# Expert gates of a product-key layer: each token's gates built once for all 128 second keys beside the first product's blocks, instead of twice for 64 keys each

## Chip, cores, metric

One NeuronCore of a Trainium2 chip runs the whole program. The metric is device time in microseconds, the median of three runs; lower is better.

## What is computed

The program is a two-block sequence model on 256 tokens of width 1024, float32. The change touches one part of it, the product-key expert layer ("PEER"), which runs three times: for both token streams in layer 0 and for one in layer 1. For each token and each of 8 heads it finds 16 of 16,384 experts:

```
s = einsum("thpd,hpnd->thpn", q, sub_keys)         # 128 first and 128 second keys
st, it = top_k(s, 16); cand = st[..,0,:,None] + st[..,1,None,:]
best, pos = top_k(cand, 16); e = it0 * 128 + it1 at pos; g = softmax(best)
act = gelu(einsum("thkd,td->thk", u[e], t))
out = einsum("thk,thkd->td", g * act, v[e])
```

## The kernel before

The kernel gathers nothing. It streams all of U and V (128 blocks of 128 experts by 1024 each, 512 KB a block) through a ring of 4 slots, computes the activations of all 16,384 experts for all 256 tokens, multiplies them by gates that are zero except for the chosen experts, and multiplies by V. One run of the layer is one phase of the program, in which each engine has its own instruction list and waits on semaphores:

- **Cells.** `S` holds, per partition (first key), a row per second key `c` and in it 256 tokens. Block `c` of U gives row `c`.
- **Blocks.** ScalarE rounds each block to float32r (`high`, L1870, 3 buffers), another engine subtracts to get the rest (`low`), TensorE multiplies the parts. In U (`up`, L1748 to L1750: 24 matmuls of 256 columns a block) `low` is GpSimd's (L1733); in V (`down`, L1800 to L1804: 12 matmuls of 512 columns) it is VectorE's (L2044), which also splits the cell row (`split`, L2037) after ScalarE rounded it (`weights`, L1925).
- **Gelu.** ScalarE turns the product of each U block into row `c` (`gelu`, L1875), and rounds the next ring block right after it. PSUM banks 4 to 7 take the blocks in turn, so `up` may run at most 4 blocks ahead of it.
- **Top-k.** VectorE finds the 16 experts per head beside the first U blocks. Its scratch lies in the rows 64 to 127 of `S`. TensorE turns the result (first keys, second keys, weights of 128 hits per token) around, `turn_found` at L1776, once after block 39 and once after block 51, and ScalarE copies it to `R` (`keep_found`, L1890).
- **Gates.** A gate matrix of one token is the product of two one-hot matrices over its 128 hits, `hotA` (first keys) and `hotB` (second keys times weight). VectorE makes both (`hot`: L2014 compares second keys, L2017 first keys, L2020 multiplies by the weight), TensorE multiplies (`build`, L1786), VectorE multiplies the cells by the result in PSUM (`gate`, L2030). A group is 8 tokens by 64 second keys, one PSUM bank. The 32 groups of second keys 0 to 63 are built beside U blocks 64 to 127, one before every two blocks. The 32 groups of keys 64 to 127 are built beside V blocks 0 to 63 in the same way, with the same `hotA` made again, because those cells are only ready when U is done.
- **Order.** It is written out by hand: TensorE's list decides which build stands before which block, and each engine's list is in program order. A list that stops at a wait holds everything behind it.

## Time and profile before

| | |
|---|---|
| median of 3 runs | 4347.95 us (4345.4 to 4363.05) |
| the profiled execution | 4347.48 us, its span 4345.6 us |
| TensorE busy | 4012.2 us, 92% |
| VectorE busy | 2377.6 us, 55% |
| ScalarE busy | 1645.8 us, 38% |
| GpSimd busy | 1399.2 us, 32% |
| mean granted TensorE clock | 0.955 of full |

The three runs of the layer take the stretches from about 1335 to 2213 us, 2238 to 3115 us and 3445 to 4323 us of the span. A profile row gives the start and the length of an instruction, the engine, the line of the kernel, the tiles, and in brackets how long the engine sat idle before it and what released it. PE is TensorE's matmul, PEld its weight load, DVE is VectorE, ACT is ScalarE, POOL is GpSimd. A float32 matmul appears as two instructions, and their ends are modelled, so the pace is read from one start to the next. A row of stretches gives the stretch, its length, the busy time (and instructions) of PE, PEld, DVE, ACT and POOL, the granted clock, the DMA share and GB/s.

### The profile page before, as it was taken

Reading aid. Unit: us, or ns where it says so; the run is one execution under the profiler, and the core shown is the slowest. Engines: PE = TensorE matmul, PEld = TensorE weight load, DVE = VectorE, ACT = ScalarE, POOL = GpSimd, SP = SyncE. Lnnn points to the kernel's source line nnn. Section 1 sums busy time; section 2 is a strip of 40 time slices with the busy share of each in tenths; the row PEclk is TensorE's granted clock in tenths of the full one; section 3 lists DMA queues with packets and bytes.
Section 4 is the critical chain, followed back from the end, with each engine's and each line's share of the span. In section 5 each row is a group of like instructions: output and inputs, shape, how many; then the busy total and the mean of one; then the engine's idle time right before and its main releaser. Section 6 shows DMA issues by size and latency. Waiting matters only on the chain. (4 is left out here: it accounts for less than half of the span.)

```text
span 4345.6 us, 71586 instructions
## 1 busy us (share of the span) xinstructions
PE 4012.2 (92%) x25466; PEld 3534.9 (81%) x25466; DVE 2377.6 (55%) x4173; ACT 1645.8 (38%) x2573; POOL 1399.2 (32%) x555
## 2 busy tenths in 40 slices
PE   7997798978988999999989999999788799999998
PEld 7973388967657999988879999888676799998887
DVE  4012413145535766687549466885555295667855
ACT  3532203232324443334544433334433344333344
POOL 5840006400005976300038865000000288660000
PEclk9998899989889999999999999999888899999999
DMA  5565544522004554444645544446421255444454
GB/s 188 179 214 194 193 136 150 167 87 73 24 25 131 165 156 140 136 145 155 193 141 169 161 140 134 144 144 192 140 89 39 88 162 166 141 136 141 145 183 150
DMA packets 168400, 614.28 MB, mean 141 GB/s; under 512 B 18593, under 2 KB 20001, under 8 KB 167969
## 3 DMA queue, kind: packets, MB, share of 16 engines
q1 hardware_dynamic: 168224, 611.88, 45.1%
q8 instruction: 117, 1.92, 0.2%
q14 instruction: 59, 0.48, 0.0%
HBM read 610.76 MB, written 1.05 MB: 141 GB/s over the span
## 5 line engine op out<-in xcount | busy, mean ns | idle before, releaser
L1733 POOL TENSOR_TENSOR ring_r<-ring,ring_hi 128x1024 fp32r<-128x1024 f32 x408 | 1073.2, 2638 | 1435.5 <-ACT ring_hi L1870 1434.8
L1870 ACT ACTIVATE ring_hi<-ring 128x1024 fp32r<-128x1024 f32 x792 | 837.8, 1059 | 822.8 <-DMA ring<-in_peer_v 485.9
L1748 PE MATMUL bank<-H_r,ring_hi 128*128 128x256 f32 x3264 | 938.2, 287 | 65.3 <-POOL ring_r L1733 63.1
L1749 PE MATMUL bank<-H_r,ring_hi 128*128 128x256 f32 x3264 | 925.5, 284 | 0.0
L1750 PE MATMUL bank<-H_r,ring_r 128*128 128x256 f32 x3264 | 925.0, 283 | 0.0
L1748 PEld LDWEIGHTS bank<-H_r,ring_hi 128*128 128x128 f32 x3264 | 627.8, 192 | 73.6 <-POOL ring_r L1733 45.6
L1749 PEld LDWEIGHTS bank<-H_r,ring_hi 128*128 128x128 f32 x3264 | 628.2, 192 | 0.0
L1750 PEld LDWEIGHTS bank<-H_r,ring_r 128*128 128x128 f32 x3264 | 627.8, 192 | 0.0
L1800 PE MATMUL bank<-ring_hi,H_r 128*128 128x512 f32 x1536 | 484.6, 397 | 4.7 <-DVE ring_r L2044 4.6
L280 POOL TENSOR_TENSOR ring_r<-ring,ring_hi 128x1024 fp32r<-128x1024 f32 x133 | 319.2, 2402 | 495.3 <-ACT ring_hi L274 494.8
L1802 PE MATMUL bank<-ring_r,H_r 128*128 128x512 f32 x1536 | 475.6, 391 | 0.0
L1804 PE MATMUL bank<-ring_hi,H_r 128*128 128x512 f32 x1536 | 475.1, 391 | 0.0
L2044 DVE TENSOR_TENSOR ring_r<-ring,ring_hi 128x1024 fp32r<-128x1024 f32 x384 | 467.9, 1219 | 0.0
L290 PE MATMUL bank<-H_r,ring_hi 128*128 128x256 f32 (+1 forms) x1464 | 455.3, 311 | 0.0
L1875 ACT ACTIVATE arena<-bank 128x256 f32 (+1 forms) x384 | 147.6, 384 | 638.3 <-PE bank L1750 637.9
L1786 PEld LDWEIGHTS bank<-arena 128*128 128x128 f32 x3072 | 365.5, 192 | 9.1 <-ACT arena L1875 2.0
L1786 PE MATMUL bank<-arena 128*128 128x64 f32 x3072 | 363.6, 271 | 1.4 <-ACT arena L1875 1.4
L2030 DVE TENSOR_TENSOR arena<-arena,bank 128x512 f32 x192 | 132.1, 688 | 414.0 <-PE bank L1786 413.8
L2014 DVE TENSOR_TENSOR arena<-CS,arena 128x512 f32<-128x512 f32 x192 | 308.9, 1609 | 88.6 <-ACT arena L1890 88.6
L1802 PEld LDWEIGHTS bank<-ring_r,H_r 128*128 128x128 f32 x1536 | 289.4, 188 | 61.8
L1804 PEld LDWEIGHTS bank<-ring_hi,H_r 128*128 128x128 f32 x1536 | 289.5, 188 | 61.3
L289 PE MATMUL bank<-H_r,ring_hi 128*128 128x256 f32 x1064 | 303.7, 285 | 29.4 <-POOL ring_r L280 29.4
(313 smaller groups left out, 5525.5 us busy)
## 6 DMA issues: line engine op xcount, KB each, us to landing
ring<-in_peer_u SPq DMA_DIRECT2D x384, 512.0 KB, 3.6
ring<-in_peer_v SPq DMA_DIRECT2D x384, 512.0 KB, 3.6
ring<-in_w_in SPq DMA_DIRECT2D x135, 512.0 KB, 3.7
ring<-in_ada SPq DMA_DIRECT2D x96, 512.0 KB, 5.1
ring<-in_w_f SPq DMA_DIRECT2D x72, 512.0 KB, 4.2
ring<-in_w_br SPq DMA_DIRECT2D x24, 512.0 KB, 3.7
ring<-in_w_q SPq DMA_DIRECT2D x24, 512.0 KB, 3.6
ring<-in_w_out SPq DMA_DIRECT2D x16, 512.0 KB, 3.6
```

The source lines that it names most:

```text
L280: eng.tensor_tensor(ring_lo[:, slot, :], ring[:, slot, :], ring_hi[:, m % NH, :].bitcast(F32), ALU.subtract).then_inc(lows, 1)
L290: pe.matmul(o, hi[:, k], x_lo(kt), start=False, stop=False)
L1733: pool.tensor_tensor(ring_lo[:, slot, :], ring[:, slot, :], ring_hi[:, m % NH, :].bitcast(F32), ALU.subtract).then_inc(p_lo, 1)
L1748: pe.matmul(o, hi[:, k], x_hi_[:, kt, :], start=(kt == 0), stop=False)
L1749: pe.matmul(o, hi[:, k], x_lo_[:, kt, :], start=False, stop=False)
L1750: mm = pe.matmul(o, lo[:, k], x_hi_[:, kt, :], start=False, stop=(kt == KT - 1))
L1786: mm = pe.matmul(o[:, u * 64:(u + 1) * 64], hotA[:, g % 2, u, :], hotB[:, g % 2, u, :], start=True, stop=True)
L1800: pe.matmul(bank[2 * t + e][:, :], w_hi, hi[:, v], start=start, stop=False)
L1802: pe.matmul(bank[2 * t + e][:, :], w_hi, lo[:, v], start=False, stop=False)
L1804: mm = pe.matmul(bank[2 * t + e][:, :], w_lo, hi[:, v], start=False, stop=stop)
L1870: act.activation(ring_hi[:, m % NH, :], ring[:, (n0 + m) % NS, :], ACT.Copy).then_inc(a_hi, 1)
L2044: dve.tensor_tensor(ring_lo[:, slot, :], ring[:, slot, :], ring_hi[:, m % NH, :].bitcast(F32), ALU.subtract).then_inc(v_lo, 1)
```

## The change

The gates are built once per token, for all 128 second keys, and all beside U. A group ("quad") is now 4 tokens by 128 keys, so it fills one PSUM bank as before; there are 64 of them. Quad `q` is built before U block `48 + floor(1.25 q)`, so 4 of every 5 blocks from 48 on have one. Because cells beyond the current block hold no activation yet, a cell holds either an activation or a gate:

- rows below the block's number: VectorE multiplies them by the gate (`gate`);
- rows from it on: ScalarE copies the gate into the cells (`keep_rest`), and when the activation of row `c` arrives, ScalarE writes the part for tokens whose gates are there to a side buffer `late` and the part for the other tokens to `S` (`gelu_late`), and VectorE multiplies the side buffer in (`gate_late`).

The one-hot of the first keys is made by VectorE for even quads and by ScalarE for odd ones (`hot_rows`: 1 - |row - k|, cut at zero). `low` of U blocks 48 to 127 moves from GpSimd to VectorE (`low_up`). The second `turn_found` moves from after block 51 to after block 47, right before the first build. V is one stream of 128 blocks with no builds, gates or one-hots in it. The loops over blocks 48 to 127 are written out.

The diff, cut to its core (the split loops of the V part, joined into one, are left out):

```diff
-    hotA = A.take(2, 8, P)
-    hotB = A.take(2, 8, NK // 2)
+    hotA = A.take(2, 4, P)
+    hotB = A.take(2, 4, P)
+    late = A.take(4, T)
...
+    C0, QUADS = 48, T // 4
+    first_row = [C0 + q * (NK - C0) // QUADS for q in range(QUADS)]
+    def quads_at(c):
+        return [q for q in range(QUADS) if first_row[q] == c]
+    def built(c):
+        return sum(f <= c for f in first_row)
...
-            with pool.Fori(0, 11) as it:
+            with pool.Fori(0, 4) as it:
                 for m in range(12):
                     low(m, it)
-            for m in range(132, v0):
+            for m in range(48, u0 + C0):
...
-                pe.wait_ge(p_lo, turns(it, u0 + c + 1))
+                if it is None and c >= C0:
+                    pe.wait_ge(v_ulo, c - C0 + 1)
+                else:
+                    pe.wait_ge(p_lo, turns(it, u0 + c + 1))
...
+            def build(q):
+                pe.wait_ge(v_hot, q + 1)
+                if q % 2:
+                    pe.wait_ge(a_hot, q // 2 + 1)
+                if q >= 4:
+                    pe.wait_ge(a_rest, q - 3)
+                for u in range(4):
+                    mm = pe.matmul(bank[q % 4][:, u * P:(u + 1) * P], hotA[:, q % 2, u, :], hotB[:, q % 2, u, :],
                                    start=True, stop=True)
                 mm.then_inc(g_ps, 1)
...
+            for c in range(40, C0):
+                up(c)
...
+            for c in range(C0, NK):
+                for q in quads_at(c):
+                    build(q)
+                up(c)
+            for c in range(4):
+                down(c)
+            with pe.Fori(0, 9) as it:
+                for c in range(4, 16):
+                    down(c, it)
+            for c in range(112, NK):
...
+            def gelu_late(c):
+                t = 4 * built(c)
+                act.wait_ge(blocks_done, n0 + u0 + c + 1)
+                if c >= C0 + 4:
+                    act.wait_ge(v_late, c - C0 - 3)
+                g = act.activation(late[:, c % 4, 0:t], bank[4 + c % 4][:, 0:t], ACT.Gelu)
+                if t < T:
+                    g = act.activation(S[:, c, t:], bank[4 + c % 4][:, t:T], ACT.Gelu)
+                g.then_inc(a_gelu, 1)
+                high(u0 + c + NH)
+            def keep_rest(q):
+                act.wait_ge(v_g, q + 1)
+                f = first_row[q]
+                act.activation(S[:, f:, 4 * q:4 * q + 4],
+                               bank[q % 4][:, :].rearrange("p (t k) -> p k t", t=4)[:, f:, :],
+                               ACT.Copy).then_inc(a_rest, 1)
+            def hot_rows(q):
+                act.wait_ge(a_t, TT)
+                if q >= 2:
+                    act.wait_ge(g_ps, q - 1)
+                for u in range(4):
+                    w = act.activation(hotA[:, q % 2, u, :], cc("iota"), ACT.Abs, scale=-1.0,
+                                       bias=rows_[:, 4 * q + u:4 * q + u + 1])
+                link(w)
+                act.activation(hotA[:, q % 2, :, :], hotA[:, q % 2, :, :], ACT.Relu, scale=-1.0,
+                               bias=1.0).then_inc(a_hot, 1)
+            hot_rows(1)
+            for c in range(C0, NK):
+                gelu_late(c)
+                for q in quads_at(c):
+                    keep_rest(q)
+                    if q % 2 and q + 2 < QUADS:
+                        hot_rows(q + 2)
...
+            def hit_keys(q):
+                if q >= 2:
+                    dve.wait_ge(g_ps, q - 1)
+                r = slice(4 * q, 4 * q + 4)
+                dve.tensor_tensor(hotB[:, q % 2, :, :], cc("iota").unsqueeze(1).to_broadcast([P, 4, P]),
+                                  cols_[:, r].unsqueeze(2).to_broadcast([P, 4, P]), ALU.is_equal).then_inc(v_col, 1)
+            def weigh_keys(q):
+                r = slice(4 * q, 4 * q + 4)
+                if q % 2 == 0:
+                    dve.tensor_tensor(hotA[:, q % 2, :, :], cc("iota").unsqueeze(1).to_broadcast([P, 4, P]),
+                                      rows_[:, r].unsqueeze(2).to_broadcast([P, 4, P]), ALU.is_equal)
+                dve.wait_ge(v_col, q + 1)
+                dve.tensor_tensor(hotB[:, q % 2, :, :], hotB[:, q % 2, :, :],
+                                  wts[:, r].unsqueeze(2).to_broadcast([P, 4, P]), ALU.mult).then_inc(v_hot, 1)
+            def gate(q):
+                f = first_row[q]
+                dve.wait_ge(g_ps, q + 1)
+                dve.wait_ge(a_gelu, f)
+                w = S[:, 0:f, 4 * q:4 * q + 4]
+                o = bank[q % 4][:, :].rearrange("p (t k) -> p k t", t=4)[:, 0:f, :]
                 dve.tensor_tensor(w, w, o, ALU.mult).then_inc(v_g, 1)
+            def gate_late(c):
+                t = 4 * built(c)
+                dve.wait_ge(a_gelu, c + 1)
+                dve.wait_ge(a_rest, built(c))
+                dve.tensor_tensor(S[:, c, 0:t], S[:, c, 0:t], late[:, c % 4, 0:t], ALU.mult).then_inc(v_late, 1)
+            def low_up(c):
+                m = u0 + c
+                dve.wait_ge(a_hi, m + 1)
+                slot = (n0 + m) % NS
+                dve.tensor_tensor(ring_lo[:, slot, :], ring[:, slot, :], ring_hi[:, m % NH, :].bitcast(F32),
+                                  ALU.subtract).then_inc(v_ulo, 1)
...
+            low_up(C0)
             dve.wait_ge(a_t, TT)
-            hot(0)
-            hot(1)
-            dve.wait_ge(a_gelu, HALF)
-            with dve.Fori(0, 5) as it:
-                for i in range(6):
-                    gate(i, it)
-                    hot(i + 2, it)
-            gate(30)
-            hot(32)
-            gate(31)
-            hot(33)
-            dve.wait_ge(v_g, 32)
+            for q in range(2):
+                hit_keys(q)
+                weigh_keys(q)
+            low_up(C0 + 1)
+            for c in range(C0, NK):
+                quads = quads_at(c)
+                for q in quads:
+                    gate(q)
+                    if q + 2 < QUADS:
+                        hit_keys(q + 2)
+                if c + 2 < NK:
+                    low_up(c + 2)
+                for q in quads:
+                    if q + 2 < QUADS:
+                        weigh_keys(q + 2)
+                if c > C0:
+                    gate_late(c - 1)
+            gate_late(NK - 1)```

VectorE's list beside U, from the loop body before (the compare of second keys, the compare of first keys, the multiplication by weights, the gate; ISA and REGISTER_ALU rows set loop addresses):

```order
L2030 TENSOR_TENSOR arena<-arena,bank 128x64x8
L2014 ISA
L2014 TENSOR_TENSOR arena<-CS,arena 128x512
L2017 ISA
L2017 TENSOR_TENSOR arena<-CS,arena 128x1024
L2019 REGISTER_ALU
L2020 ISA
L2020 TENSOR_TENSOR arena<-arena 128x512
```

and after, for U blocks 95, 96 and 97 (L2055 gate, L2037 second keys, L2067 `low` of a U block, L2043 first keys, L2046 weights, L2061 the late row):

```order
L2055 TENSOR_TENSOR arena<-arena,bank 128x95x4
L2037 TENSOR_TENSOR arena<-CS,arena 128x512
L2067 TENSOR_TENSOR ring_r<-ring,ring_hi 128x1024
L2043 TENSOR_TENSOR arena<-CS,arena 128x512
L2046 TENSOR_TENSOR arena<-arena 128x512
L2061 TENSOR_TENSOR arena<-arena 128x152
L2055 TENSOR_TENSOR arena<-arena,bank 128x96x4
L2037 TENSOR_TENSOR arena<-CS,arena 128x512
L2067 TENSOR_TENSOR ring_r<-ring,ring_hi 128x1024
L2046 TENSOR_TENSOR arena<-arena 128x512
L2061 TENSOR_TENSOR arena<-arena 128x156
L2067 TENSOR_TENSOR ring_r<-ring,ring_hi 128x1024
```

The list had four operations for every two blocks; it now has five or six for a block with a quad and two for one without.

ScalarE's list beside U after the change, from the end of block 51 (L1921 and L1923 the two parts of the activation, L1865 the rounding, L1930 the copied gates, L1939 and L1942 the one-hot of four tokens; before, the list only alternated between L1875 and L1870):

```order
L1939 ACTIVATE arena<-CS,arena 128x128 x4
L1942 ACTIVATE arena<-arena 128x512
L1921 ACTIVATE arena<-bank 128x16
L1923 ACTIVATE arena<-bank 128x240
L1865 ACTIVATE ring_hi<-ring 128x1024
L1921 ACTIVATE arena<-bank 128x20
L1923 ACTIVATE arena<-bank 128x236
L1865 ACTIVATE ring_hi<-ring 128x1024
L1930 ACTIVATE arena<-bank 128x75x4
```

No instruction that loads an activation table stands between them.

## Rows read from the trace of the kernel before

**Rows 1.** The page's part 1: busy time, share of the span, instructions.
```profile
PE 4012.2 (92%) x25466; PEld 3534.9 (81%) x25466; DVE 2377.6 (55%) x4173; ACT 1645.8 (38%) x2573; POOL 1399.2 (32%) x555
```
**Rows 2.** Busy time of each engine in five stretches of the layer's first run.
```profile
1514.60:1560.70 46.10, 45.99 (x384) 45.79 (x383) 17.78 (x6) 23.44 (x33) 41.34 (x17) 1.00 0.59 178
1560.70:1802.20 241.50, 241.50 (x2055) 241.45 (x2053) 157.66 (x128) 88.76 (x128) 160.92 (x63) 1.00 0.45 140
1802.20:1806.40 4.20, 2.15 (x18) 1.86 (x16) 1.61 (x3) 2.36 (x5) 0.00 (x0) 1.00 0.54 161
1806.40:2038.60 232.20, 232.19 (x1264) 200.85 (x1265) 187.49 (x252) 86.25 (x126) 0.00 (x0) 0.99 0.46 142
2038.60:2213.10 174.50, 174.50 (x769) 143.95 (x768) 97.42 (x125) 84.69 (x124) 0.00 (x0) 1.00 0.63 193
```
**Rows 3.** The timeline of PE beside U, two builds: start us, length, instruction.
```profile
1704.35 1.89 PE L1786 MATMUL bank<-arena 128*128 128x64 f32 x16
1706.05 0.36 PE L1748 MATMUL bank<-H_r,ring_hi 128*128 128x256 f32 x1
...
1711.88 1.89 PE L1786 MATMUL bank<-arena 128*128 128x64 f32 x16
```
**Rows 4.** The timeline of PE beside V, with builds and without.
```profile
2002.36 1.89 PE L1786 MATMUL bank<-arena 128*128 128x64 f32 x16
...
2009.62 1.89 PE L1786 MATMUL bank<-arena 128*128 128x64 f32 x16
...
2040.02 0.62 PE L1800 MATMUL bank<-ring_hi,H_r 128*128 128x512 f32 x2
...
2042.74 0.62 PE L1800 MATMUL bank<-ring_hi,H_r 128*128 128x512 f32 x2
```
**Rows 5.** The timeline of PE in an earlier phase, float32 matmuls of 128 columns.
```profile
1155.39 0.39 PE L1445 MATMUL bank<-arena 128*128 128x128 f32 x2
1155.61 0.39 PE L1444 MATMUL bank<-arena 128*128 128x128 f32 x2
```
**Rows 6.** The timeline of DVE beside V, where GpSimd is idle.
```profile
1997.14 0.69 DVE L2030 TENSOR_TENSOR arena<-arena,bank 128x512 f32 x1 [1.29 <-PE bank L1786]
1997.75 0.68 DVE L2014 TENSOR_TENSOR arena<-CS,arena 128x512 f32<-128x512 f32 x1
1998.35 1.22 DVE L2017 TENSOR_TENSOR arena<-CS,arena 128x1024 f32<-128x1024 f32 x1
1999.49 0.68 DVE L2020 TENSOR_TENSOR arena<-arena 128x512 f32<-128x512 f32 x1
2000.09 0.42 DVE L2037 TENSOR_TENSOR H_r<-arena,H_r 128x256 fp32r<-128x256 f32 x1
2000.42 1.22 DVE L2044 TENSOR_TENSOR ring_r<-ring,ring_hi 128x1024 fp32r<-128x1024 f32 x1
```
**Rows 7.** The timeline after the second turn of the top-k result, all engines.
```profile
1526.11 0.49 PE L1776 MATMUL bank<-CS,arena 128*128 128x128 f32 x3
...
1528.10 1.06 ACT L1870 ACTIVATE ring_hi<-ring 128x1024 fp32r<-128x1024 f32 x1 [1.41 <-DMA ring<-in_peer_u]
1529.07 0.47 ACT L1890 ACTIVATE arena<-bank 128x384 f32<-128x384 f32 x1
...
1529.57 2.62 DVE L2014 TENSOR_TENSOR arena<-CS,arena 128x512 f32<-128x512 f32 x1 [29.92 <-ACT arena L1890]
```
**Rows 8.** The timeline from U to V.
```profile
1802.39 0.38 ACT L1875 ACTIVATE arena<-bank 128x256 f32<-128x256 f32 x1 [1.54 <-PE bank L1750]
...
1804.79 0.43 DVE L2037 TENSOR_TENSOR H_r<-arena,H_r 128x256 fp32r<-128x256 f32 x1 [5.17 <-ACT H_r L1925]
1805.13 1.22 DVE L2044 TENSOR_TENSOR ring_r<-ring,ring_hi 128x1024 fp32r<-128x1024 f32 x1
...
1806.40 0.73 PE L1800 MATMUL bank<-ring_hi,H_r 128*128 128x512 f32 x2 [1.58 <-DVE ring_r L2044]
```
**Rows 9.** Groups by line on ACT, an activation with a bias column.
```profile
L385 ACT ACTIVATE h_high<-H,MODS 128x256 fp32r<-128x256 f32 x32 | 13.2, 496 | 8.7 <-DVE H L403 8.7
```

More of the change, by code:

```diff
@@ L1777, in turn_found @@
                             mm.then_inc(t_ps, 1)
-                        def build(g, it=None):
-                            n = g if it is None else it * 6 + g
-                            pe.wait_ge(v_hot, n + 1)
-                            if it is not None or g not in (0, 1, 32, 33):
-                                pe.wait_ge(v_g, n - 1)
-                            o = bank[(0 if g < 32 else 4) + g % 2]
-                            for u in range(8):
-                                mm = pe.matmul(o[:, u * 64:(u + 1) * 64], hotA[:, g % 2, u, :], hotB[:, g % 2, u, :],
+                        def build(q):
[6 more added lines that the diff above has]
+                                mm = pe.matmul(bank[q % 4][:, u * P:(u + 1) * P], hotA[:, q % 2, u, :], hotB[:, q % 2, u, :],
                                                start=True, stop=True)
@@ L1915, in _ @@
                         keep_found(0)
-                        gelu_turns(3, 4)
+                        for c in range(40, C0):
+                            gelu(c)
                         keep_found(1)
-                        gelu_turns(4, 10)
-                        for c in range(124, NK):
-                            gelu(c)
+                        link = linker(act, a_chain)
+                        def gelu_late(c):
[8 more added lines that the diff above has]
+                            high(u0 + c + NH)
@@ L1934, in _ @@
                                 high(v0 + NH + c, it)
-                        for c in range(60, 62):
-                            weights(2 + c)
-                            high(v0 + NH + c)
-                        act.wait_ge(v_g, 64)
-                        with act.Fori(0, 5) as it:
-                            for c in range(62, 74):
-                                weights(2 + c, it)
-                                high(v0 + NH + c, it)
-                        for c in range(122, 126):
+                        for c in range(120, 126):
                             weights(2 + c)
@@ L2056, in _ @@
-                        hot(32)
-                        gate(31)
-                        hot(33)
-                        dve.wait_ge(v_g, 32)
-                        dve.wait_ge(blocks_done, n0 + v0)
-                        dve.wait_ge(a_gelu, NK)
-                        with dve.Fori(0, 5) as it:
-                            for i in range(6):
-                                split(2 * i, it)
-                                low(2 * i, it)
-                                split(2 * i + 1, it)
-                                low(2 * i + 1, it)
-                                gate(32 + i, it)
-                                hot(34 + i, it)
@@ L2071, in _ @@
-                        for i in (30, 31):
-                            split(2 * i)
-                            low(2 * i)
-                            split(2 * i + 1)
-                            low(2 * i + 1)
-                            gate(32 + i)
-                        dve.wait_ge(v_g, 64)
-                        with dve.Fori(0, 5) as it:
-                            for i in range(12):
-                                split(HALF + i, it)
-                                low(HALF + i, it)
@@ L2083, in _ @@
-                        for c in range(HALF + 60, NK):
+                        for q in range(2):
[15 more added lines that the diff above has]
+                                gate_late(c - 1)
@@ L2084, in _ @@
+                        gate_late(NK - 1)
+                        dve.wait_ge(blocks_done, n0 + v0)
+                        with dve.Fori(0, 10) as it:
+                            for c in range(12):
+                                split(c, it)
+                                low(c, it)
+                        for c in range(120, NK):
                             split(c)
```

60 lines of the change are left out of this document (6 added, 54 removed).

## The prediction, made before the changed kernel ran

> **What bounds the kernel now.** I read the busy shares first: TensorE is busy 92% of the span, no other engine more than 55% [rows 1]. Then the stretches [rows 2], which cover the changed part of one run of the layer: U blocks 48 to 63, U blocks 64 to 127 with 32 builds, the passage to V, V blocks 0 to 63 with 31 builds, V blocks 64 to 127. In all but the passage TensorE has no idle time at all and the clock is granted in full (0.99 and 1.00), while VectorE and ScalarE have some. So here the time is the sum of TensorE's list. The timelines then price that list. A U block without a build takes 46.1 / 16 = 2.88 us [rows 2]; two blocks and a build beside U take 1711.88 - 1704.35 = 7.53 us [rows 3], so a build costs 7.53 - 2 x 2.88 = 1.77. A V block takes 2042.74 - 2040.02 = 2.72; two and a build take 7.26 [rows 4], so a build costs 1.82. A build is 16 instructions, 8 float32 matmuls of 64 columns, at 0.11 us each. The five stretches sum to 698.5 us; the other two runs of the layer repeat them.
>
> **Builds on TensorE: the gain.** A quad has 4 matmuls of 128 columns instead of 8 of 64. The nearest row is an earlier phase's float32 matmul of 128 columns: 1155.61 - 1155.39 = 0.22 us for two instructions, 0.11 each [rows 5]. The same as with 64 columns, so what costs is the instruction and not its columns. A quad takes 8 x 0.112 = 0.90 us. Removed beside V: 31 x 1.82 = 56.4 us. Beside U: 64 x 0.90 = 57.6 instead of 32 x 1.77 = 56.6, so +1.0. Bounds: 0.90 if the pace of the rows holds, 1.0 if each quad pays an edge of 0.1 on entering and leaving; +6 per layer at most.
>
> **The first build: a new stall.** The second turn of the top-k result now stands right before the first build, so a chain that used to run beside 12 U blocks is exposed. Before, the turn started at 1526.11, and ScalarE copied the result at 1529.07 to 1529.54 only, since it was behind the rounding of a block that waited 1.41 us for its DMA [rows 7]: 3.4 us. The same list stands before it now (the activation of block 47, the rounding, the copy). In the better case, with the block already there, about 2 us. Then VectorE compares second keys, compares first keys and multiplies, each on 512 elements: 0.6 + 0.6 + 0.68, counting from start to start [rows 6]. The compare took 2.62 us in rows 7 with GpSimd at work; GpSimd's last U block is now 47, so I take the length without it. With a handover of 0.1 us the stall is 5.1 on the mean of both cases, at least 4.0, at most 9 if GpSimd still interferes. The idle time costs clock as well: in the V stretch 232.2 us are listed where 64 x 2.72 + 31 x 1.82 = 230.5 are explained, after a passage with 2.1 us of PE idle and at a clock of 0.99 [rows 2]; that is 1.7 us. I take 2. Together +7 us per layer.
>
> **VectorE beside U.** It gains `low` of 80 blocks and the late rows, and loses half of the first-key compares. Over five blocks with four quads near the end of U, where gates and late rows are longest: 5 `low` of 1.22, 4 gates of up to 0.69, 4 compares and 4 multiplications of 0.68, 2 first-key compares of 0.68 (each 512 elements; before, 1024 at 1.22), 5 late rows of up to 0.42 (256 elements) [rows 6]: 6.1 + 2.8 + 5.4 + 1.4 + 2.1 = 17.8 us by listed lengths. Consecutive rows start 0.08 us before the listed end of the last (1997.14 + 0.69 against 1997.75), so 24 operations take 15.9. TensorE needs 5 x 2.88 + 4 x 0.90 = 18.0. It is covered, by 2 us of 18 at the end of U and by 4 to 5 at block 48. The order matters too: `low` of block c + 2 and the weights of quad q + 2 stand in the list behind the gate that waits for build q. From the end of build q they need 0.4 for the handover, then gate, compare, `low`, first keys, weights: 0.6 + 0.6 + 1.14 + 0.6 + 0.68 = 3.6, so 4.0; TensorE asks for them 2.9 + 3.8 = 6.7 us after that end. Cost zero; without that cover, a block would wait for VectorE.
>
> **ScalarE beside U.** Per block an activation in two parts, about 0.53 for both (0.38 for 256 [rows 8] and a second fixed part of 0.15), and 1.06 for the rounding [rows 7]. Per quad the copy of the gates, at most 0.40 (the 384 columns of rows 7 took 0.47). Per odd quad four activations of 128 with a bias column: one of 256 took 0.496 [rows 9], less 128 elements gives 0.38 each, and one of 512, about 0.60. Five blocks sum to 2.7 + 5.3 + 1.6 + 3.0 + 1.2 = 13.8 of 18.0 us. But the one-hot of quad q + 2 is made only after block c: from its end 0.2 + 0.35 + 0.96 + 0.35 + 4 x 0.29 + 0.1 + 0.7 = 3.8 us from start to start, and the build that needs it starts 3.78 us later where no bare block lies between, which is the case for every second odd quad. I take a stall of 0.2 us for 16 of them, +3 us per layer; bounds 0 and 1 us each, so 0 to +16. No table load stands in the new list; one per change of function would have sunk this.
>
> **GpSimd** ends its work 80 blocks earlier; nothing waits for it. **DMA** is read in V at 193 GB/s in the last stretch without one idle slice of TensorE [rows 2]; the same pace now holds for 128 blocks. Cost zero. **The passage to V**, 4.2 us, was the chain activation, rounding, splitting, `low` (1802.39 to 1806.40) [rows 8]; a build lay inside it and cost nothing. The chain stays, with one late row of 0.42 beside the rounding: no gain and no loss, up to +2 for clock as the idle time is now in one piece.
>
> **Sum.** Per layer -56.4 + 1.0 + 7 + 3 = -45.4 us; three times: -136. Against the profiled execution of 4347.5 us (0.5 below the median) that gives **4212 us**. Its own range: 4181 if neither the stall nor the lateness shows (-55.4 x 3), 4245 with 9 us at the first build, 1.0 a quad, and some lateness of ScalarE.
>
> **Rivals.** (1) *VectorE becomes the bound of U.* For it: only 2 us of 18 are free at the end, and gates now touch 4 cells in a row (16 bytes) instead of 8. Against it: the gate over strided cells and a transposed bank took 0.69, the contiguous compare 0.68 [rows 6], so stride costs nothing yet. If the operations did not overlap and the four gates took twice as long, five blocks would need 17.8 + 2.8 = 20.6 us instead of 18.0: +2.6 x 16 = 42 per layer, **4338 us**; with the gates alone hurt, some 4250. The Trainium skill, page "SBUF — State Buffer", section "Specifications (TRN2)", says that an access pattern loses bandwidth when it does not make at least two hits in each 16-byte line, and that PSUM lines hold two float32; by that rule the transposed read of the bank should already be dear before the change, and this trace does not agree (0.69 against 0.68).
>
> (2) *ScalarE's one-hots come late.* If an activation of 128 does not overlap the next, or the copy of gates over rows of 4 cells takes twice its length, the chain is 4.8 instead of 3.8: +1 us for 16 to 32 quads, some 4260 to **4300 us**.
>
> (3) *Slower than before.* The lead of two quads does not hold: build q + 1 waits for weights that VectorE makes only after build q, because its list (gate, compare, `low`, first keys, weights) stands behind that build. A quad then costs 0.90 + 4.0 = 4.9 us instead of 3.78: +1.1 x 64 = 70 per layer, less 45: 3 x 25 = +75, **4423 us**. It decides from the point where each quad loses more than 45.4 / 64 = 0.7 us, so where that chain exceeds 3.6 us with a lead of one or 7.4 us with the lead of two that the list gives. It is 4.0 by the rows; to reach 7.4 its operations must be slowed by four fifths. GpSimd did more than that to the compare of rows 7 (2.62 for 0.68), but it is silent there.
>
> **Chances.** The forecast's case 0.78; rival 1 0.08 (most of it near 4250 to 4300); rival 2 0.09; rival 3 0.03; a gain smaller for another reason 0.02. The range takes the first case whole and the near half of rivals 1 and 2: 4180 to 4258. About 0.5% (22 us) is what a measurement of this kernel can tell from no change. Faster by more: 0.94 (case 1, rival 2, most of rival 1); within: 0.03; slower: 0.03.
>
> **What would show it.** Right: in the stretch of V 128 blocks at 2.72 us with DMA near 193 GB/s; a quad's 8 instructions taking 0.90 us; two blocks with quads 7.56 us apart; one idle gap of 4 to 6 us before the first build; VectorE near 88% busy at the end of U, its compares at 0.68. Wrong: PE rows beside U that name VectorE's `low` or weights, or ScalarE's one-hot, as releaser in block after block (rivals 1 to 3), a quad at 1.7 us (no gain on TensorE), or gaps in V that name a DMA.

## The result, and the profile after

The changed kernel takes **4207.11 us** (median of 4 runs, 4205.31 to 4210.37) against 4349.91 us for the kernel before in the same session: ratio 0.9668, 95% interval 0.9646 to 0.969. That is 3.3% faster, and 5 us from the forecast. The profiled execution has a span of 4202.5 us at a mean granted clock of 0.951. Busy shares, which answer to [rows 1]:

```profile
PE 3850.9 (92%) x23930; PEld 3374.3 (80%) x23930; DVE 2306.9 (55%) x4557; ACT 1853.7 (44%) x3479; POOL 780.8 (19%) x315
```

TensorE has 161 us less work and the same share: it still sets the time. The stretches of the layer's first run, which answer to [rows 2] (first build; the 4.4 us behind it; start of block 48 to start of block 127; from there to the first V block; V block 0; all of V):

```profile
1527.69:1529.04 1.35, 1.35 (x9) 1.35 (x9) 1.31 (x3) 0.00 (x0) 0.00 (x0) 0.66 0.00 0
1529.04:1533.42 4.38, 4.38 (x30) 4.38 (x29) 4.26 (x6) 0.13 (x2) 0.00 (x0) 0.71 0.02 4
1529.04:1815.08 286.04, 285.20 (x2403) 284.69 (x2403) 232.57 (x376) 176.08 (x452) 0.00 (x0) 1.00 0.48 144
1815.08:1822.01 6.93, 3.03 (x26) 2.83 (x25) 2.46 (x5) 3.87 (x8) 0.00 (x0) 0.98 0.48 151
1822.01:1826.29 4.28, 4.28 (x12) 3.42 (x13) 2.89 (x4) 0.00 (x0) 0.00 (x0) 0.64 0.00 0
1822.01:2171.90 349.89, 349.89 (x1536) 289.26 (x1536) 198.07 (x254) 170.72 (x250) 0.00 (x0) 1.00 0.63 190
```

V is now 349.89 us with no idle time, at 190 GB/s. Before it was 406.7. Where a stretch shows less than full clock (0.64 to 0.71), it stands right behind an idle gap of TensorE. The granted clock has two levels, 1.2 and 2.4 GHz, so such a mean says that part of the stretch ran at the lower one.

TensorE's timeline beside U, against [rows 3], and beside V, against [rows 4]:

```profile
1573.02 1.05 PE L1801 MATMUL bank<-arena 128*128 128x128 f32 x8
1573.83 0.36 PE L1760 MATMUL bank<-H_r,ring_hi 128*128 128x256 f32 x1
...
1583.54 1.05 PE L1801 MATMUL bank<-arena 128*128 128x128 f32 x8
...
1587.30 1.05 PE L1801 MATMUL bank<-arena 128*128 128x128 f32 x8
...
2001.74 0.62 PE L1815 MATMUL bank<-ring_hi,H_r 128*128 128x512 f32 x2
...
2004.46 0.62 PE L1815 MATMUL bank<-ring_hi,H_r 128*128 128x512 f32 x2
```

A block with a quad takes 1587.30 - 1583.54 = 3.76 us, so a quad costs 3.76 - 2.88 = 0.88. A block without one still takes 2.88. A V block takes 2004.46 - 2001.74 = 2.72 (this form stands twice in a block; the one between is left out). The way to the first build, all engines, against [rows 7] (L1791 turns the top-k result, L1885 copies it, L2037, L2043 and L2046 make the one-hots of a quad):

```profile
1523.28 0.49 PE L1791 MATMUL bank<-CS,arena 128*128 128x128 f32 x3
1523.48 0.38 ACT L1870 ACTIVATE arena<-bank 128x256 f32<-128x256 f32 x1 [1.00 <-PE bank L1762]
1524.27 1.06 ACT L1865 ACTIVATE ring_hi<-ring 128x1024 fp32r<-128x1024 f32 x1 [0.41 <-DMA ring<-in_peer_u]
1525.23 0.47 ACT L1885 ACTIVATE arena<-bank 128x384 f32<-128x384 f32 x1
1525.74 0.69 DVE L2037 TENSOR_TENSOR arena<-CS,arena 128x512 f32<-128x512 f32 x1 [4.79 <-ACT arena L1885]
1526.35 0.69 DVE L2043 TENSOR_TENSOR arena<-CS,arena 128x512 f32<-128x512 f32 x1
1526.95 0.68 DVE L2046 TENSOR_TENSOR arena<-arena 128x512 f32<-128x512 f32 x1
1527.69 1.70 PE L1801 MATMUL bank<-arena 128*128 128x128 f32 x8 [3.92 <-DVE arena L2046]
```

From the turn to the build are 4.41 us; 3.92 of them TensorE is idle. The compare takes 0.69 where it took 2.62 beside GpSimd. Last, VectorE's four largest groups by line from 1529 to 1818 us, and ScalarE's one-hots (count, busy us, mean ns, then the idle time before them and who ended it):

```profile
L2067 DVE TENSOR_TENSOR ring_r<-ring,ring_hi 128x1024 fp32r<-128x1024 f32 x79 | 96.5, 1221 | 19.4 <-ACT ring_hi L1865 19.4
L2046 DVE TENSOR_TENSOR arena<-arena 128x512 f32<-128x512 f32 x62 | 42.5, 685 | 0.0
L2037 DVE TENSOR_TENSOR arena<-CS,arena 128x512 f32<-128x512 f32 x62 | 42.5, 685 | 0.0
L2055 DVE TENSOR_TENSOR arena<-arena,bank 128x192 f32<-128x192 f32 (+31 forms) x64 | 33.0, 516 | 32.5 <-PE bank L1801 23.1 <-ACT arena L1923 8.9
...
L1939 ACT ACTIVATE arena<-CS,arena 128x128 f32<-128x128 f32 x124 | 39.7, 406 | 0.0
```

VectorE still waits for others (32.5 us before its gates, 19.4 before `low`), and in the blocks behind the first build nobody waits for it. The profile lists one wait of TensorE there, 0.84 us at the build before block 91. ScalarE's rounding was held by a ring block that landed late, and the copied gates and the one-hot of an odd quad stand behind that rounding in ScalarE's list:

```profile
1682.61 1.06 ACT L1865 ACTIVATE ring_hi<-ring 128x1024 fp32r<-128x1024 f32 x1 [0.95 <-DMA ring<-in_peer_u]
...
1685.79 1.13 PE L1801 MATMUL bank<-arena 128*128 128x128 f32 x8 [0.84 <-issue]
```

The profile names no releaser for that wait. By the lists it is the one-hot of quad 35, which ended at 1685.69; the weights of that quad had been ready since 1681.21. The experiments on the first keys below bear it out.

**By layer.** From the first U block to the end of V the three runs took 852.6, 852.9 and 853.2 us before and take 804.2, 802.2 and 803.3 now: 49.7 us less on the mean. Three times that is 149; the two profiled spans differ by 143. The other 6 us lie outside the layer. Its first run starts at 1342.45 us instead of 1335.29, and in the profiles of the twelve kernels below it starts anywhere from 1328.5 to 1344.3, with the same code ahead of it. So that difference is scatter and no effect of the change.

### The profile page after: what moved, and what is told of

Read it like the earlier page. It is cut to its first block and busy times, and to the rows that moved or that the text cites. A ratio compares the mean times of both kernels' runs of the same rounds, so it can differ in the third digit from the quotient of the medians.

```text
span 4202.5 us, 68036 instructions
## 1 busy us (share of the span) xinstructions
PE 3850.9 (92%) x23930; PEld 3374.3 (80%) x23930; DVE 2306.9 (55%) x4557; ACT 1853.7 (44%) x3479; POOL 780.8 (19%) x315
## 3 DMA queue, kind: packets, MB, share of 16 engines
q8 instruction: 150, 2.46, 0.2%
HBM read 610.76 MB, written 1.05 MB: 146 GB/s over the span
## 5 line engine op out<-in xcount | busy, mean ns | idle before, releaser
L1865 ACT ACTIVATE ring_hi<-ring 128x1024 fp32r<-128x1024 f32 x792 | 839.2, 1060 | 597.8 <-DMA ring<-in_peer_v 506.9
L1760 PE MATMUL bank<-H_r,ring_hi 128*128 128x256 f32 x3264 | 947.8, 290 | 64.6 <-POOL ring_r L1745 62.5
L1762 PE MATMUL bank<-H_r,ring_r 128*128 128x256 f32 x3264 | 926.6, 284 | 0.0
L1745 POOL TENSOR_TENSOR ring_r<-ring,ring_hi 128x1024 fp32r<-128x1024 f32 x168 | 454.9, 2722 | 1434.5 <-ACT ring_hi L1865 1433.8
L1760 PEld LDWEIGHTS bank<-H_r,ring_hi 128*128 128x128 f32 x3264 | 630.0, 193 | 72.5 <-POOL ring_r L1745 45.0
L1761 PEld LDWEIGHTS bank<-H_r,ring_hi 128*128 128x128 f32 x3264 | 630.4, 193 | 0.0
L1762 PEld LDWEIGHTS bank<-H_r,ring_r 128*128 128x128 f32 x3264 | 629.3, 193 | 0.0
L1815 PE MATMUL bank<-ring_hi,H_r 128*128 128x512 f32 x1536 | 475.4, 391 | 12.7 <-DVE ring_r L2082 12.7
L1819 PE MATMUL bank<-ring_hi,H_r 128*128 128x512 f32 x1536 | 474.4, 390 | 0.0
L2082 DVE TENSOR_TENSOR ring_r<-ring,ring_hi 128x1024 fp32r<-128x1024 f32 x384 | 467.9, 1219 | 0.0
L280 POOL TENSOR_TENSOR ring_r<-ring,ring_hi 128x1024 fp32r<-128x1024 f32 x133 | 318.9, 2401 | 499.9 <-ACT ring_hi L274 499.3
L2075 DVE TENSOR_TENSOR H_r<-arena,H_r 128x256 fp32r<-128x256 f32 x384 | 163.4, 425 | 449.8 <-ACT H_r L1956 430.2
L1815 PEld LDWEIGHTS bank<-ring_hi,H_r 128*128 128x128 f32 x1536 | 289.3, 189 | 74.1 <-DVE ring_r L2082 14.1
L2067 DVE TENSOR_TENSOR ring_r<-ring,ring_hi 128x1024 fp32r<-128x1024 f32 x240 | 293.0, 1221 | 92.7 <-ACT ring_hi L1865 92.7
L1819 PEld LDWEIGHTS bank<-ring_hi,H_r 128*128 128x128 f32 x1536 | 289.2, 188 | 60.2
L291 PE MATMUL bank<-H_r,ring_r 128*128 128x256 f32 x1064 | 304.3, 286 | 0.0
L290 PEld LDWEIGHTS bank<-H_r,ring_hi 128*128 128x128 f32 x1464 | 289.9, 198 | 14.3
```

The source lines that it names most:

```text
L280: eng.tensor_tensor(ring_lo[:, slot, :], ring[:, slot, :], ring_hi[:, m % NH, :].bitcast(F32), ALU.subtract).then_inc(lows, 1)
L290: pe.matmul(o, hi[:, k], x_lo(kt), start=False, stop=False)
L1745: pool.tensor_tensor(ring_lo[:, slot, :], ring[:, slot, :], ring_hi[:, m % NH, :].bitcast(F32), ALU.subtract).then_inc(p_lo, 1)
L1760: pe.matmul(o, hi[:, k], x_hi_[:, kt, :], start=(kt == 0), stop=False)
L1761: pe.matmul(o, hi[:, k], x_lo_[:, kt, :], start=False, stop=False)
L1762: mm = pe.matmul(o, lo[:, k], x_hi_[:, kt, :], start=False, stop=(kt == KT - 1))
```

## The experiments

The theory after the result: TensorE's list is all that counts, the instruction and not its columns sets the price of a build, and what is left to gain are three small stalls (first build, odd quads, entry to V). The rivals: VectorE or ScalarE are nearly the bound, or GpSimd's silence is what made it work. The base run again:

> The changed kernel once more, as the base for the three kernels beside it: 4207 us within 0.1%.

Measured 4206.31 us (5 runs, 4203.2 to 4208.14), ratio 0.9665. The kernels below are compared with this.

**Price by instruction.** `cols64` splits each build matmul in two of 64 columns: the same products in twice the instructions.

```diff
-    mm = pe.matmul(bank[q % 4][:, u * P:(u + 1) * P], hotA[:, q % 2, u, :], hotB[:, q % 2, u, :], ...)
+    for e in range(2):
+        mm = pe.matmul(bank[q % 4][:, u * P + 64 * e:u * P + 64 * e + 64], hotA[:, q % 2, u, :],
+                       hotB[:, q % 2, u, 64 * e:64 * e + 64], ...)
```

> Each matmul of a quad's build is split into two of 64 second keys: 8 matmuls instead of 4, the same columns and the same work for every other engine. If a build costs by the instruction (0.11 us each), a quad goes from 0.88 to 1.77 us: +0.88 x 64 x 3 = +169, so 4376 us, and the gain of the change is gone. Rival: the gain comes from the other engines (VectorE freed of GpSimd's interference and of the second making of the one-hots, V as one stream), and TensorE's builds only filled gaps: then 4207 to 4230 us.

Measured 4364.47 us (8 runs), ratio 1.0034 (1.002 to 1.0048): the whole gain is gone. It is 12 us under the forecast of 4376. TensorE's timeline beside U:

```profile
1578.58 1.89 PE L1802 MATMUL bank<-arena 128*128 128x64 f32 x16
...
1583.23 1.89 PE L1802 MATMUL bank<-arena 128*128 128x64 f32 x16
```

A block with a quad takes 4.65, so a quad 1.77, exactly a build of [rows 3] and twice the 0.88. The layout of the gates, the move to U and the stream of V are all kept here, and V still takes 350 us. So it is the number of float32 matmul instructions that the change gains by; the rest of it only has to keep TensorE from waiting. The 5 us per layer by which this kernel is slower than the one before (857.9 against 852.9) are about the new stall at the first build. Blocks 48 to 127 take 340.2 us instead of 286, 54 us more where the forecast had 56; part of that is that every block with a quad, behind block 48, takes 4.65 and none is late for ScalarE.

**The first build.** `turn_early` turns and copies the top-k result after block 43 instead of 47, and VectorE makes `low` behind the weights of each of the first two quads.

```diff
-    for c in range(40, C0):
+    for c in range(40, 44):
         up(c)
     turn_found(1)
+    for c in range(44, C0):
+        up(c)
```

> The second turn of the top-k result and its copy stand after block 43 instead of after block 47, and VectorE's first low_up behind the first quad's weights. If the gap before the first build is the exposed chain turn, copy, compare, first keys, weights (4.9 to 5.3 us, plus about 1 us of half clock behind it), it disappears in all three layers: -6 x 3 = -18, so 4189 us. VectorE's operations then run beside GpSimd, each up to 2.9 us, so some 2 us per layer may stay: 4195. Rival: the gap is waiting for something else at that place (the weights arrive late because of VectorE's own list, or a block of U): then the gap stays where it is or moves, and the time stays at 4207.

Measured 4190.63 us (5 runs, 4188.57 to 4197.61), ratio 0.9635. Blocks 0 to 48 take 156.05, 155.3 and 155.4 us instead of 161.4, 159.7 and 160.2: the stall was worth 5 us per layer. The block behind the first build still takes 4.11 to 4.67 instead of 3.76, since ScalarE makes the one-hot of quad 1 only behind its work on block 47.

**Who makes the first keys.** `keys_dve` gives all of them to VectorE, `keys_act` all to ScalarE, `early_dve` joins `keys_dve` and `turn_early`.

```diff
-    if q % 2 == 0:
-        dve.tensor_tensor(hotA[:, q % 2, :, :], ..., ALU.is_equal)
+    dve.tensor_tensor(hotA[:, q % 2, :, :], ..., ALU.is_equal)
...
-    if q % 2 and q + 2 < QUADS:
-        hot_rows(q + 2)
```

> VectorE makes the first-key one-hot of all quads, ScalarE of none. If VectorE is covered as forecast, its list grows by 2 x 0.6 to 17.1 us of 17.9 in five blocks near the end of U and to some 14.4 at block 48, TensorE still waits for nothing, and the 0.1 to 0.2 us of ScalarE's lateness in one of five blocks goes: 4204 us (-3). Rival: the half on ScalarE is what keeps VectorE from being the bound; then the last third of U's blocks waits for it, +0.1 to 0.5 us a block: 4215 to 4240.

> ScalarE makes the first-key one-hot of all quads. Its list grows from 13.8 to about 17.8 us of listed lengths in five blocks (17.9 for TensorE), some 15.5 from start to start. From the end of a block to its one-hot are 3.8 to 3.95 us, and the next but one build asks for it 3.76 us later unless a bare block lies between: three quads of four wait 0.1 to 0.2 us instead of one in four, and the delay may add up from block to block: +0.5 us in five blocks, +8 per layer, 4232 us. If the delays add up because the list is full: 4300.

> Both: the early turn and all first-key one-hots on VectorE. If the two effects are independent, -18 - 3: 4186 us. If VectorE needs the time it lost to GpSimd in blocks 44 to 47 back, it starts block 48 behind and the sum is smaller: 4195.

Measured: `keys_dve` 4202.56 us (5 runs, 4200.31 to 4210.61), `keys_act` 4209.95 (2 runs), `early_dve` 4188.89 (5 runs, 4182.16 to 4190.79). The runs of `keys_dve` overlap those of the base, and those of `early_dve` overlap those of `turn_early`, so these 2 to 4 us are not shown by the times. The intervals between blocks show the effect. In the change, one block in five is late, the one ahead of every second odd quad: 3.96, 3.90, 3.88, 3.86 and so on down to 3.78 instead of 3.76, about 0.8 us per layer. `keys_dve` has 3.76 throughout, behind block 48. `keys_act` missed its forecast of 4232: in its profile it is still one block in five that is late (3.96, 3.90, 3.88 and so on), now the one ahead of an even quad. The delays do not add up. A late build also puts off the request for the next one-hot, which is then in time; that is read from the list and was not tested.

Single blocks are late by more, and for another cause, the late ring blocks seen above. Where ScalarE makes one-hots, its waits for DMA reach TensorE: block 90 takes 4.84 us in the change (ScalarE waited 0.95) and 4.79 in the base run again (0.90), and `keys_act` has blocks of 5.39, 4.94 and 4.72 us behind waits of 1.52, 1.07 and 0.82. In `keys_dve` and `early_dve` ScalarE waits for DMA just as long (up to 0.92 and 1.06 us), and not one block from 49 on is late. So moving the one-hots to VectorE takes ScalarE's DMA waits off TensorE's path, besides the 0.8 us. Why the 0.8 us fades can be read in ScalarE's timeline of the change, in the copies of the gates, of which every second stands ahead of a one-hot (the first, the one at block 84, the one at block 126):

```profile
1534.57 0.44 ACT L1930 ACTIVATE arena<-bank 128x320 f32<-128x320 f32 x1
...
1664.55 0.32 ACT L1930 ACTIVATE arena<-bank 128x176 f32<-128x176 f32 x1
...
1816.68 0.16 ACT L1930 ACTIVATE arena<-bank 128x8 f32<-128x8 f32 x1
```

It covers only the rows from the block on, so it shortens by 20 elements every five blocks, from 0.44 us at first to 0.16, 0.12 us less by block 84. The lateness falls at about that pace, 0.02 us every five blocks. That reading was not tested by itself. In `early_dve` the first builds stand 3.76 us apart:

```profile
1524.89 1.05 PE L1799 MATMUL bank<-arena 128*128 128x128 f32 x8
...
1528.65 1.05 PE L1799 MATMUL bank<-arena 128*128 128x128 f32 x8
```

**GpSimd's silence.** `low_pool` gives `low` of U blocks 48 to 127 back to GpSimd and takes it from VectorE.

```diff
-    with pool.Fori(0, 4) as it:
+    with pool.Fori(0, 11) as it:
         for m in range(12):
             low(m, it)
-    for m in range(48, u0 + C0):
+    for m in range(132, v0):
         low(m)
...
-    low_up(c + 2)
```

> low of U blocks 48 to 127 is GpSimd's again, as before the change; VectorE loses 5 x 1.14 us of its 15.9 in five blocks, but its operations with two inputs in SBUF run beside GpSimd. Before the change one in three or four of them took 2.5 instead of 0.68 us. If one per quad does: 10.2 + 4 x 1.85 = 17.6 of 17.9 us, at the bound: 4207 to 4240 us, with waits for the weights at the end of U. Rival: every one of them is held for 2.4 us or more; then a quad takes over 6 us and VectorE sets the pace of U: 4500 us and more. Second rival: moving low was not needed at all: 4207 or less.

Measured 4282.9 us (2 runs), ratio 0.9839 (0.9811 to 0.9868): 77 us slower than the change and 43 above the top of what was expected, between the forecast and its first rival. VectorE has 96.5 us of work less per layer and is slower for it. Its groups by line from 1526 to 1836 us, and TensorE's builds from 1529 to 1836 us:

```profile
L2043 DVE TENSOR_TENSOR arena<-arena 128x512 f32<-128x512 f32 x62 | 117.6, 1896 | 1.1
L2034 DVE TENSOR_TENSOR arena<-CS,arena 128x512 f32<-128x512 f32 x62 | 79.7, 1286 | 0.0
L2058 DVE TENSOR_TENSOR arena<-arena 128x4 f32<-128x4 f32 (+38 forms) x78 | 55.4, 723 | 1.2 <-ACT arena L1927 1.2
L2040 DVE TENSOR_TENSOR arena<-CS,arena 128x512 f32<-128x512 f32 x31 | 36.5, 1177 | 0.0
L2052 DVE TENSOR_TENSOR arena<-arena,bank 128x192 f32<-128x192 f32 (+31 forms) x64 | 32.3, 505 | 4.0 <-PE bank L1798 3.9
...
L1798 PE MATMUL bank<-arena 128*128 128x128 f32 x504 | 69.5, 282 | 17.1 <-DVE arena L2043 16.9
```

Every operation of VectorE that reads two operands from SBUF has a longer mean: the multiplication by weights 1896 ns instead of 685, the compares 1286 and 1177, the late rows 723 instead of 288. The gate, which reads one operand from PSUM, has not changed (505 against 516). TensorE is idle 17 us per layer before builds, and the releaser named is the multiplication by weights, not GpSimd's `low`. From start to start, blocks 48 to 127 take 309.9 us instead of 286.0. The kernel before shows the same two things beside U, from 1560 to 1802 us:

```profile
L2014 DVE TENSOR_TENSOR arena<-CS,arena 128x512 f32<-128x512 f32 x32 | 76.1, 2378 | 0.0
L2030 DVE TENSOR_TENSOR arena<-arena,bank 128x512 f32 (+1 forms) x32 | 22.0, 688 | 94.6 <-PE bank L1786 94.5
```

Beside V, where GpSimd is idle, the same compare has a mean of 684 ns and the gate again 688. In `low_pool` the timeline shows one such meeting:

```profile
1707.23 0.68 DVE L2034 TENSOR_TENSOR arena<-CS,arena 128x512 f32<-128x512 f32 x1
1707.33 2.84 POOL L1745 TENSOR_TENSOR ring_r<-ring,ring_hi 128x1024 fp32r<-128x1024 f32 x1 [1.85 <-ACT ring_hi L1862]
1707.95 2.78 DVE L2043 TENSOR_TENSOR arena<-arena 128x512 f32<-128x512 f32 x1
```

The multiplication that meets a running subtraction of GpSimd is listed with 2.78 us and ends at 1710.73, after GpSimd's at 1710.17. The Trainium skill, page "SBUF — State Buffer", section "SBUF: two separate sides", says that a VectorE operation with two SBUF inputs and a GpSimd operation that reads SBUF exclude each other for a whole instruction. This trace agrees: 2.78 and 2.89 us for operations of 0.68 that have both inputs in SBUF, and no such delay for the gate.

**A lead of one quad.** `lead_one` is `keys_dve` with the one-hots of quad q + 1, not q + 2, behind gate q. It makes the condition of the prediction's third rival true.

```diff
-    if q + 2 < QUADS:
-        hit_keys(q + 2)
+    if q + 1 < QUADS:
+        hit_keys(q + 1)
...
-    if q + 2 < QUADS:
-        weigh_keys(q + 2)
+    if q + 1 < QUADS:
+        weigh_keys(q + 1)
```

> On the kernel with all first-key one-hots on VectorE (4203 us): the compares and weights that stand behind the gate of quad q are those of quad q + 1 instead of q + 2. This makes the condition of the prediction's third rival true. From the end of a build VectorE then needs 0.4 + 0.35 to 0.6 + 0.6 + 1.14 + 0.6 + 0.68 = 3.8 to 4.0 us to the weights of the next quad, TensorE asks for them 2.88 us after that end, or 5.76 where a bare block lies between. If the chain is what the rows say, 48 of 64 quads wait 0.9 to 1.1 us: +48 per layer, 4350 us. If VectorE's chain does not matter because TensorE's builds have other slack: 4203.

Measured 4338.65 us (6 runs), ratio 0.9968 (0.9948 to 0.9987). TensorE's timeline, then VectorE's:

```profile
1610.52 1.16 PE L1799 MATMUL bank<-arena 128*128 128x128 f32 x8 [0.60 <-DVE arena L2040]
...
1615.15 1.16 PE L1799 MATMUL bank<-arena 128*128 128x128 f32 x8 [0.60 <-DVE arena L2040]
```

```profile
1611.71 0.44 DVE L2049 TENSOR_TENSOR arena<-arena,bank 128x276 f32<-128x276 f32 x1 [1.11 <-PE bank L1799]
1612.07 0.69 DVE L2032 TENSOR_TENSOR arena<-CS,arena 128x512 f32<-128x512 f32 x1
1612.67 1.22 DVE L2061 TENSOR_TENSOR ring_r<-ring,ring_hi 128x1024 fp32r<-128x1024 f32 x1
1613.81 0.69 DVE L2037 TENSOR_TENSOR arena<-CS,arena 128x512 f32<-128x512 f32 x1
1614.41 0.68 DVE L2040 TENSOR_TENSOR arena<-arena 128x512 f32<-128x512 f32 x1
```

Build, gate, compare, `low`, first keys, weights, build: each stands behind the last, 4.63 us around, growing from 4.55 to 4.87 with the gate. Only the quad behind a bare block escapes (3.69). So the two-quad lead is worth 136 us of the kernel (4338.65 - 4202.56), nearly the whole gain of 147.

**A later start.** `start64_dve` starts the builds at block 64, with a quad before every block from there on, turns after block 59, and leaves all first keys to VectorE. `start64` is the same with half on ScalarE.

```diff
-    C0, QUADS = 48, T // 4
+    C0, QUADS = 64, T // 4
```

> Builds start at U block 64, one before every block and no bare block between; the second turn stands after block 59, so no gap before the first build; all first-key one-hots on VectorE. TensorE's list is the same, 4189 us if it waits for nothing. VectorE needs per block gate 0.5 to 0.6, compare 0.6, low 1.14, first keys 0.6, weights 0.6 to 0.7, late row 0.1 to 0.34: 3.6 us at block 64, 3.9 at block 127, against 3.76 of TensorE. It is past its cover only in the last third: +0.1 us for some 20 to 30 blocks, 4192 to 4200 us. If the cover is smaller than the rows say (rival 1 of the prediction), the loss starts at block 64 and grows: 4230 and more.

> The same with half of the first-key one-hots on ScalarE. VectorE needs 3.3 to 3.6 us per block and is covered. Every odd quad's one-hot is asked for 3.76 us after the end of the block two before, and takes 3.75 to 3.95: the lateness of 0.0 to 0.2 us falls on 32 quads instead of 16, smaller as the gate copy shrinks with later rows: +2 per layer against start64 without waits, 4195 us. If all waits of the changed kernel come from bare blocks and their absence instead of from this chain, 4189.

Measured 4184.22 and 4196.1 us (2 runs each). The first was better than expected (4192 to 4200): every block keeps 3.76 us, although VectorE's list was reckoned longer than that. `combined` below shows how it fits. The second met its forecast of 4195, but not by the lateness of 0.0 to 0.2 us alone: that adds up to 0.8 us in the first run of its layer, and six single blocks add 2.9, the longest 4.91 us behind a wait of ScalarE for DMA of 1.03.

**The entry to V, and the fastest version.** `v_entry` is `early_dve` in which VectorE makes `low` of V blocks 0 and 1 ahead of its last late row, and ScalarE rounds cell rows 0 and 1 ahead of a ring block. `combined` is `start64_dve` with the same entry.

```diff
+    low(0)
+    low(1)
     gate_late(NK - 1)
     dve.wait_ge(blocks_done, n0 + v0)
...
     act.wait_ge(v_g, QUADS)
-    act.wait_ge(v_late, NK - C0)
     weights(0)
     weights(1)
+    high(v0 + NH - 1)
+    act.wait_ge(v_late, NK - C0)
```

> On the early turn with all one-hots on VectorE (4189 us): low of V blocks 0 and 1 stands before the last late row, and ScalarE rounds the cell rows 0 and 1 before the ring block that comes after the last activation. The passage to V is the chain activation 127, rounding, cell rounding, split, low of 4.0 us with up to 2 us of half clock behind it; left of it are the cell rounding and the split. TensorE's gap falls from 4.0 to some 1.3 us and the clock stays full: -2.7 - 1.5 = -4.2 per layer, 4176 us. Rival: the passage waits for the DMA of V's blocks; then the gap stays: 4189.

> The start at block 64 with a quad before every block and all first keys on VectorE (4184.2 us alone), with the entry to V of the 4175.4 us run. If both gains are independent, the entry's 13.5 us (4188.9 to 4175.4) come off the 4184.2: 4171 us, with U127 to V0 5.2 to 5.8 us and every block with a quad 3.76. The rival: with a quad before every block VectorE has less spare time at the end of U (start to start 19.6 of 18.8 us by listed lengths in five blocks), so the two early subtractions of V put it behind and the entry gains nothing: 4184 us, passage at 7 us.

Measured: `v_entry` 4175.38 us (5 runs, 4170.6 to 4178.81), ratio 0.9592; `combined` **4168.8 us** (5 runs, 4167.34 to 4174.03), ratio 0.9584 (0.9571 to 0.9598), the fastest of all. From block 127 to V block 0 are 5.82, 5.21 and 5.21 us in `v_entry` and 4.81, 4.60 and 4.60 in `combined`, about 7.0 in the change. The clock goes with it. First `combined`: U blocks 64 to 127 as a stretch, V's beginning as a stretch. Then `v_entry`'s first V block:

```profile
1566.97:1804.66 237.69, 237.69 (x2027) 237.69 (x2025) 228.80 (x374) 99.08 (x252) 0.00 (x0) 1.00 0.46 141
1809.47:1813.30 3.83, 3.83 (x17) 3.16 (x18) 1.75 (x3) 1.44 (x3) 0.00 (x0) 1.00 0.30 112
```

```profile
1805.47:1809.87 4.40, 4.40 (x13) 3.52 (x14) 1.75 (x3) 0.23 (x1) 0.00 (x0) 0.62 0.08 32
```

`combined` keeps the full clock behind an idle time of 1.70 us, and its first V block takes 2.84 us. `v_entry` was idle for 2.77 us and pays 4.4 us for that block at 0.62. The other two layer runs agree: 1.49 and 1.50 us idle in `combined` with first blocks of 2.83 and 2.85, 2.18 us idle twice in `v_entry` with first blocks of 4.23 and 4.41. The first stretch also shows VectorE busy 228.80 of 237.69 us, 96%. Near the end of U its own rows (gates, L2053) stand 3.83 and 3.84 apart:

```profile
1790.20 0.66 DVE L2053 TENSOR_TENSOR arena<-arena,bank 128x492 f32<-128x492 f32 x1
...
1794.03 0.66 DVE L2053 TENSOR_TENSOR arena<-arena,bank 128x496 f32<-128x496 f32 x1
...
1797.87 0.67 DVE L2053 TENSOR_TENSOR arena<-arena,bank 128x500 f32<-128x500 f32 x1
```

There VectorE is slower than TensorE by 0.08 us a block, and the lead of two quads takes it up until U ends. A longer U should show it; none was run.

## Why the prediction was right, and where not

- **Gain beside V.** Predicted -56.4 us per layer, measured 406.7 to 350.4, -56.3. `cols64` shows the reason given: two instructions of 0.11 us per matmul, with 64 or 128 columns. V's entry is at half clock in both (4.2 to 4.5 us for its first block), so the difference is free of it.
- **Quads beside U.** Predicted +1.0 (0.90 each), measured 0.88 each: 64 x 0.88 - 32 x 1.77 = -0.3. The upper bound of 1.0 a quad was not needed.
- **First build.** Predicted 5.1 for the chain and 2 for the clock. The two cases that the 5.1 is called the mean of (5.4 and 4.0 with the same terms) have a mean of 4.7, so the term was 0.4 too high by its own working. Measured are 4.41, 4.44 and 4.49 us from the turn to the build. The chain was the one predicted. The clock behind it takes its share in two places: from the build to the block's matmuls are 1.35, 1.73 and 1.72 us instead of 0.81, and block 48 takes 4.86, 4.38 and 5.22 instead of 3.76. Together that is 1.5 to 2.4 us, 1.9 on the mean, close to the 2. In the first run block 48 is late by clock alone, since the one-hot of quad 1 was ready at 1527.68. The interval between blocks 47 and 48 is 8.64, 9.05 and 9.09 us.
- **ScalarE's lateness.** Predicted 0.2 us for 16 quads, +3. The place was right (every second odd quad, the one without a bare block ahead). The size was 0.20 only at the first and fell to nothing by block 90, 0.8 in all. The term took a chain of constant length, with the copy of the gates at its longest, where it shortens. What it left out are late ring blocks: one adds 1.1 us in the first run of the layer. Two blocks of the third run add 0.2 us, for which no row names a cause. With these the lateness is 1.3 us on the mean.
- **VectorE.** Predicted near 88% busy and covered. In blocks 116 to 120 it is busy 15.68 of 17.92 us, 88%, and over the whole stretch from block 48 to 127 232.57 of 286.04, 81%. Strided gates cost nothing: 0.67 us for 500 elements in `combined` against 0.68 for 512 in a row, so rival 1's price does not arise.
- **GpSimd: a reason that was not priced.** "GpSimd ends its work 80 blocks earlier; nothing waits for it" put the move of `low` at nothing. `low_pool` puts it at 77 us. The forecast came out right because the durations were taken from rows without GpSimd; the sentence should have said that they hold only because it is silent. The prediction had the row that shows it (2.62 us for 0.68, [rows 7]) and used it for the first build and for rival 3, but gave it no price here.
- **Passage to V.** Predicted unchanged, measured 6.93, 7.27 and 6.82 us from block 127 to V block 0, against 7.09, 7.06 and 6.97 before. The clock's +2 did not come either: the first V block was already at 0.62 to 0.65 before the change.
- **Rival 3.** Its mechanism is real, its price was too high: `lead_one` loses 46 us per layer, not 70, since bare blocks let one quad in four escape and a block with a quad took mostly 4.55 to 4.87 us where 4.9 was reckoned, and it ends at 4338.65, not 4423. The lead held in the change, as argued.
- **Sum.** Predicted -45.4 per layer, measured -49.7. The 4.3 us between them are quads (1.3), lateness (1.8), the first build with its clock (0.8) and 0.4 in the blocks ahead of it and in rounding. 13 us over three layers would have put the time at 4199; the scatter outside the layer gave 6 back in the profile, so the 5 us of error are partly luck.

## To carry to other kernels

Price a small float32 matmul by instructions: half their number at double the columns took half the time here, from 64 to 128 columns. Wider ones were not tried. Before work is moved between VectorE and GpSimd, look at what VectorE's operations with two SBUF operands take while the other engine runs: taking 96 us per layer off VectorE made it the late one. In a list written by hand, look at the lead (how many units ahead the operands are made) before the length of any operation: one quad less of it cost 136 us with the same work. And operands for TensorE do not belong behind an operation that waits for DMA: ScalarE's one-hots passed such waits on, VectorE's did not.

## What the runs showed of the hardware that was not expected

- A VectorE operation of 0.68 us took 2.78 to 2.89 us where it met GpSimd, and the gate with one operand in PSUM did not slow at all (505 against 516 ns). Both were in the trace before (2378 ns for a compare beside U, 684 beside V; 688 for the gate in both); the second was not looked for.
- Idle gaps of TensorE of 1.49 to 1.70 us left the granted clock at 1.00, gaps of 2.18 us were followed by 4.2 to 4.4 us at 0.61 to 0.64, one of 2.77 us by 4.4 us at 0.62, and one of 3.92 us by 1.35 us at 0.66 and 4.38 at 0.71. The length of the last gap alone does not decide it: in the kernel before, gaps of 0.47 and 1.58 us with a build between them were followed by a V block at 0.65. So the last microsecond off the entry to V paid twice: about 0.6 us of idle time and 1.5 us of the first block.
- Consecutive VectorE operations overlap by about 0.08 us each, so that listed lengths overstate a full list: the largest six groups of `combined` sum to more than its stretch, while its busy time is 96% of it.
